# Overflow blocks of two mixture-of-experts layers: from one nest to groups of at most seven

## The reference, cut to what matters

```python
def hier_moe(xt, wg, bg, we, be, w1, w3, w2):
    # a group of 8 experts is chosen, in it the best TOP_K = 2 of 32 experts in all
    ...
    counts = jnp.bincount(flat_e, length=N_EXPERTS)
    ...
    def expert_block(args):
        xb, e = args
        hb = jax.nn.silu(xb @ w1[e]) * (xb @ w3[e])      # 1024 -> 512
        return hb @ w2[e]                                # 512 -> 1024
```

## Time and profile before

| | |
|---|---|
| median of 3 runs | 2109.87 us (2107.73 to 2110.74) |
| profiled execution, its own time | 2111.29 us |
| its span, first to last instruction | 2109.4 us |
| PE busy | 1954.9 us (93%) |
| DVE, ACT, POOL busy | 653.6, 370.9, 321.7 us |
| granted TensorE clock, mean | 0.992 |
| the chain that ended last | PE 69%, DMA 20%, DVE 3%, "issue" 3% |

### The profile page before, as it was taken

How to read it: one execution, slowest core, us unless ns; L and a number is a source line. 1 busy time by engine, 2 the same in 40 slices (tenths; PEclk the granted TensorE clock), 3 DMA queues, 4 the chain that set the end, 5 groups by cost and what they waited for, 6 DMA issues and landing times.

```text
span 2109.4 us, 34164 instructions
## 1 busy us (share of the span) xinstructions
PE 1954.9 (93%) x14831; PEld 1224.5 (58%) x14831; DVE 653.6 (31%) x1520; ACT 370.9 (18%) x821; POOL 321.7 (15%) x264
## 2 busy tenths in 40 slices
PE   5999999999999979999999888888789989989998
PEld 4566475555555546546565444444367677675884
DVE  1235273322222234114331111111146031037752
ACT  3133230000000002113320000000021130042131
POOL 0125402000001000114310000000120060040120
PEclk9999999999999999999999999999999999999999
DMA  9585199999999988317299999999984323427221
GB/s 362 124 274 205 56 357 381 427 426 427 426 427 422 426 347 261 118 52 281 95 381 426 427 427 426 427 426 426 407 293 151 131 81 135 145 81 200 81 92 60
DMA packets 133744, 586.23 MB, mean 278 GB/s; under 512 B 19162, under 2 KB 34474, under 8 KB 108880
## 3 DMA queue, kind: packets, MB, share of 16 engines
q1 hardware_dynamic: 117024, 558.65, 67.4%
q10 hardware_dynamic: 10448, 18.88, 3.0%
q0 software_dynamic: 6112, 6.39, 0.9%
HBM read 572.23 MB, written 25.29 MB: 283 GB/s over the span
## 4 chain that ended last, share of the span: by engine, by line
PE 69%; DMA 20%; DVE 3%; issue 3%; ACT 2%; POOL 2%; SPq 1%; DVEq 0%; POOLq 0%; ACTq 0%
DMA RG<-in_moe_w 19%; PE banks L1574 13%; PE banks L2627 8%; PE banks L1599 6%; PE banks L1550 4%; PE banks L2219 4%; PE banks L2629 4%; PE banks L1119 4%; PE banks L683 3%; PE banks L2221 3%; PE banks L2828 3%; PE banks L3039 2%; POOL AR L931 2%; PE banks L341 2%; PE banks L824 2%
## 5 line engine op out<-in xcount | busy, mean ns | idle before, releaser
L1574 PE MATMUL banks<-RG,HT 128*64 128x256 f32 x3616 | 427.8, 390 | 36.6 <-DMA RG<-in_moe_w 33.6
L1574 PEld LDWEIGHTS banks<-RG,HT 128*64 128x64 f32 x3616 | 252.6, 135 | 223.3 <-DMA RG<-in_moe_w 55.5
L1844 POOL DMA_INDIRECT y_rows<-AR x64 | 63.9, 999 | 839.8 <-DVE AR L1613 812.1
L1583 DVE TENSOR_TENSOR AR<-AR,banks 128x256 f32<-128x256 f32 x64 | 38.6, 603 | 479.6 <-ACT AR L1579 428.4
L1599 PE MATMUL banks<-RG,AR 128*64 128x512 f32 x752 | 171.7, 598 | 3.8 <-DVE AR L1592 3.1
L2627 PE MATMUL banks<-HT,RG 128*128 128x256 f32 x768 | 168.0, 380 | 0.8 <-ACT HT L550 0.8
L2627 PEld LDWEIGHTS banks<-HT,RG 128*128 128x128 f32 x768 | 145.4, 190 | 22.8 <-issue 2.4
L1579 ACT ACTIVATE AR<-banks 128x256 f32<-128x256 f32 x64 | 24.5, 383 | 744.6 <-PE banks L1574 744.6
L1550 PE MATMUL banks<-AR 128*128 128x256 bf16 (+1 forms) x1152 | 149.4, 277 | 2.0 <-DVE AR L1538 1.5
L1550 PEld LDWEIGHTS banks<-AR 128*128 128x128 bf16 x1152 | 108.3, 99 | 33.8 <-issue 18.3
L1599 PEld LDWEIGHTS banks<-RG,AR 128*64 128x64 f32 x752 | 50.0, 136 | 94.4 <-issue 83.4
(11 more groups left out here) (490 smaller groups left out, 2392.6 us busy)
## 6 DMA issues: line engine op xcount, KB each, us to landing
RG<-in_moe_w SPq DMA_DIRECT2D x160, 2048.0 KB
AR<-in_moe_w SPq DMA_DIRECT2D x32, 2048.0 KB, 21.5
RG<-in_ada_w SPq DMA_DIRECT2D x24, 2048.0 KB
RG<-in_attn_w_in SPq DMA_DIRECT2D x20, 2048.0 KB
RG<-in_odd_w_in SPq DMA_DIRECT2D x6, 2048.0 KB
RG<-in_ssm_w_in SPq DMA_DIRECT2D x4, 2048.0 KB
AR<-y_rows SPq DMA_DIRECT2D x12, 512.0 KB, 6.1
RG<-in_even_w_in SPq DMA_DIRECT2D x2, 2048.0 KB
```

Of the source, the lines that this page charges most:

```text
L1574: m = pe.matmul(p[64 * h:64 * h + 64, 256 * i:256 * i + 256], x[:, k, :], w[:, h, k], start=k == 0, stop=k == 7, skip_group_check=True)
L1844: g.indirect_dma_start(y, off, E.Y[b], None, bounds_check=2047, oob_is_err=False).then_inc(*event)
```

## The change

The nest is cut after every seventh block (`OVER = 7`). In layer 0 the 15 blocks become three nests, of 7, 7 and 1 blocks, one behind the other, each with an outer test of its own. The last block of a full group runs `over_end` without the inner test, since the code behind it is outside the nest. `sp_again` and the waits for it stand at the end of each group, inside its outer test, with a semaphore value of their own. In layer 1 there are 7 blocks, so one group, and the code is as it was. PE's part and SP's part in full:

```diff
+OVER = 7
 ...
         def pe_overflow(pe, E):
 ...
                     pe_down(pe, E, b, over_view(l, s2, 4), ev(f"over_pe{l}", "down", o))
-                    with pe.If(n < o + 2):
+                    if (o + 1) % OVER == 0:
                         over_end(pe, E, o)
-                    if o + 1 < E.no:
+                    else:
+                        with pe.If(n < o + 2):
+                            over_end(pe, E, o)
+                    if o + 1 < E.no and (o + 1) % OVER:
                         block(o + 1)
 
-            block(0)
+            for o in range(0, E.no, OVER):
+                block(o)
 ...
         def sp_overflow(sp, E):
 ...
-                    with sp.If(n < o + 2):
+                    if (o + 1) % OVER == 0:
                         over_end(sp, E, o)
-                    if o + 1 < E.no:
+                    else:
+                        with sp.If(n < o + 2):
+                            over_end(sp, E, o)
+                    if o + 1 < E.no and (o + 1) % OVER:
                         block(o + 1)
-                    if o == 0:
-                        sp_again(sp, E)
-
-            block(0)
+                    if o % OVER == 0:
+                        sp_again(sp, E, o)
+
+            for o in range(0, E.no, OVER):
+                block(o)
 ...
-        def sp_again(sp, E):
+        def sp_again(sp, E, o):
             for t in range(2):
-                sp.wait_ge(*at(f"z_load{t}", E.l, 1))
-                sp_z_load(sp, E, t, f"z_again{E.l}", t)
+                sp.wait_ge(*at(f"z_load{t}", E.l, 1) if o == 0 else at(f"z_again{E.l}{o - OVER}", 1, 1))
+                sp_z_load(sp, E, t, f"z_again{E.l}{o}", t)
```

More of the change, by code:

```diff
@@ L1937, in block @@
                     act_silu(act, E, b, ev(f"over_act{l}", "silu", o))
-                    with act.If(n < o + 2):
+                    if (o + 1) % OVER == 0:
                         over_end(act, E, o)
-                    if o + 1 < E.no:
+                    else:
+                        with act.If(n < o + 2):
+                            over_end(act, E, o)
+                    if o + 1 < E.no and (o + 1) % OVER:
                         block(o + 1)
-            block(0)
+            for o in range(0, E.no, OVER):
+                block(o)
         def dve_overflow(v, E):
@@ L1962, in block @@
                     dve_y_out(v, E, E.Y[b], b, ev(f"over_dve{l}", "y_out", o))
-                    with v.If(n < o + 2):
+                    if (o + 1) % OVER == 0:
                         over_end(v, E, o)
-                    if o + 1 < E.no:
+                    else:
+                        with v.If(n < o + 2):
+                            over_end(v, E, o)
+                    if o + 1 < E.no and (o + 1) % OVER:
                         block(o + 1)
-                    if o == 0:
-                        v.wait_ge(*at(f"z_again{l}", 1, 1))
-            block(0)
+                    if o % OVER == 0:
+                        v.wait_ge(*at(f"z_again{l}{o}", 1, 1))
+            for o in range(0, E.no, OVER):
+                block(o)
         def pool_overflow(g, E):
@@ L1983, in block @@
                             pool_gather(g, E, 34 + o, b, dm(f"over_gather{l}{b}", o + 2))
-                    if o == 0:
+                    if o % OVER == 0:
                         for t in range(2):
-                            g.wait_ge(*at(f"z_load{t}", l, 1))
+                            g.wait_ge(*at(f"z_load{t}", l, 1) if o == 0 else at(f"z_again{l}{o - OVER}", t, 1))
                     g.wait_ge(*at(f"over_dve{l}", "y_out", o))
                     pool_scatter(g, E, 32 + o, b, dm(f"over_store{l}{b}", o))
-                    with g.If(n < o + 2):
+                    if (o + 1) % OVER == 0:
                         over_end(g, E, o)
-                    if o + 1 < E.no:
+                    else:
+                        with g.If(n < o + 2):
+                            over_end(g, E, o)
+                    if o + 1 < E.no and (o + 1) % OVER:
                         block(o + 1)
-            block(0)
+            for o in range(0, E.no, OVER):
+                block(o)
         def over_view(l, slot, a):
```

## The result

| | before | after |
|---|---|---|
| median | 2108.80 us (2107.32 to 2110.74, 4 runs) | 2126.31 us (2122.06 to 2131.16, 4 runs) |
| profiled execution, its span | 2109.4 us | 2129.3 us |
| granted TensorE clock, mean | 0.992 | 0.983 |
| time ratio | | 1.0080, 95% interval 1.0068 to 1.0092 |

The change makes the kernel slower. The same kernel was timed once more in another set (first experiment) and took 2121.64 us, 12.6 more than the kernel before beside it. The forecast was 12.8 more, a time of 2122.7, in a range of 2115 to 2126.5.

What follows compares the result with a forecast made beforehand. PE, busy 93% of the span, bounds the kernel. Second jump 6.08, third 6.5, tests 0.1 and clock 0.5, less 0.4 slack, make 12.8 us more: 2122.7 us on the median of 2109.87, range 2115 to 2126.5.

Steps and rivals of the forecast that it cites:

- Where the cost lies: PE in layer 0 pays; DVE's and SP's stalls stay as they were, ACT and POOL nothing, layer 1 no change.
- First jump: PE's first outer test in layer 0, over seven blocks, into an idle queue: 3.83 us as before.
- Second jump: PE's second outer test in layer 0, over seven blocks, DMA engines full: 6.08 us, bounds 3.83 and 6.5.
- rival B: PE's second jump in layer 0 first awaits the piece behind the first's target: 19.3 us slower, 2129.2; chance 0.08.
- Third jump: PE's outer test of block 14 in layer 0 crosses a piece's start by 5 instructions: 6.5 us, bounds 0.05 and 6.5.
- Rival A: PE's third jump in layer 0 finds its target on hand: 5.8 or 3.5 us slower, 2113.4 to 2115.7; chance 0.25.
- Rival C: No slower: PE's second and third branches in layer 0 take under 0.2 us each, 2109.5 to 2110.1; chance 0.07.
- Clock and slack: Behind PE's jumps in layer 0, half clock costs 0.5 us (0 to 1); slack before L2117 hides 0.4.
- gap after 31 keeping matmuls: PE's keeping matmuls behind layer 0's jumps still stop after 31 of 72, the target 2 instructions earlier in the same piece.
- Places: In layer 0, L413's transposes at about 793.5 us and L2117's matmuls at about 805.
- Downstream: Behind L2117 nothing absorbs the delay; the DMA-bound stretch of layer 1's experts starts later by as much.

Runs made afterwards that it cites:

- PE nested again: The changed kernel with PE back in one nest, ACT, DVE, POOL and SP still in groups of seven: 1.1 us less than before, ratio 0.9996.
- eight instructions more: The changed kernel with two more keeping matmuls on PE ahead of its overflow tests in layer 0: 7.2 us more than before, ratio 1.0032.
- After again: The changed kernel, unaltered, timed once more in another set: 2121.64 us, 12.6 more than before, ratio 1.0054.
- groups of one: The kernel before with PE alone, in layer 0 alone, cut into fifteen groups of one block: 40.6 us more than before, one run.
- PE alone grouped: The kernel before with groups of seven on PE only, the other four engines in one nest: 11.3 us more than before, ratio 1.0046.
- eight and seven: The kernel before with PE alone in groups of eight and seven in layer 0 (`OVER = 8`): 7.2 us more than before, ratio 1.0032.

## Why the prediction was right

The mechanism held: the cost is PE's code, fetched at each jump whose target isn't on hand. That the sum of 12.8 came so close to the second set's 12.6 is partly luck: its terms were off by up to 1.7 us each, in both directions, and cancelled. That the first set's 2126.31 us lies in the range, 0.2 us below its end, is luck too: 17.5 us is 4.7 more than forecast, the two new stalls were only 0.6 longer than forecast in that set, and the range's upper end was made for longer stalls. Point by point:

- **Where the cost lies.** DVE, SP, ACT and POOL were forecast at nothing, shown by PE nested again. Layer 1 was forecast without change: its test takes 6.0 to 6.6 us in all these kernels, 6.08 in the earlier trace rows.
- **First jump** 3.8: 3.34 to 3.90.
- **Second jump**, the mis-sized term: 6.08 forecast from layer 1's row, 7.36 to 7.77 measured. Layer 1's jump starts with no fetch open; this one starts 3.9 us after the first, and the fetch that follows the first jump is underway beside its own. That is rival B in part: it had the two fetches in a row and gave the first a full 6.5 us, but they run side by side, and the far jump takes 1.7 to 2.4 us more than the near one's 5.69.
- **Third jump** 6.5: 5.76 to 5.84. The bound taken was the gap of the keeping matmuls; the near jump is cheaper. The two errors are +1.3 to +1.7 and -0.7, so the two new stalls together are 13.1 to 13.6 us where 12.6 were forecast.
- **Rival A** needed a third test that finds its target, and gave +5.8. With eight instructions more it came true, and the kernel took +7.2: A's sum with the second jump's right price of 7.36 is 7.1.
- **Rival C** is out: no second test over a missing piece was short. By the Trainium skill ("Advanced Engine Details and Errata", Control Flow Timing) a compare and branch is some 108 ns; PE's short ones take 219 to 378 ns here, so the row is higher, and the stalled ones show that no such figure covers them.
- **Clock and slack.** 0.5 was forecast for the clock and 0.4 gained from slack. The lower clock came, and stayed for 3.6 us after PE resumed, but it ran into something the forecast had wrong: the gap after 31 keeping matmuls, said to stay, isn't there. All 72 run in 9.62 us. The transposes and the first 32 of them take 5.72 us at a mean clock of 0.69. The next piece came 6.5 us after the resume in the earlier trace rows; here PE stops for only 0.1 us, at 799.5 and so 5.9 us after the resume. The slower matmuls reach the piece's start hardly before it is there:

```profile
793.78:799.50 5.72, 5.72 (x36) 5.72 (x36) 4.28 (x8) 1.15 (x2) 0.00 (x0) 0.69 1.05 387
799.50:804.11 4.61, 4.61 (x42) 4.57 (x42) 3.47 (x13) 1.45 (x4) 0.00 (x0) 1.00 1.06 388
```

  From the transposes to the diagonal's matmuls it takes 10.33 us, against 11.58 in the earlier trace rows. So 13.2 us of later transposes became 12.0 of later diagonal, where the forecast had 12.7 become 12.8.
- **Places.** L413 was forecast at about 793.5 and is at 793.78; L2117 at 805, and is at 804.11.
- **Downstream** nothing was to be absorbed. After again gives 11.9 us at the diagonal and 12.6 in the time, groups of one 41.1 and 40.6, one run. The weights that come late near 1192 us were not forecast; in the time of these kernels they can't be told apart. The first set's further 5 us are explained neither by the forecast nor by a run.

## What to carry to other kernels

Code that never runs has a place and a size: on an engine with a long program, count the instructions between a branch and its target, for one far jump can be cheaper than several, and a few instructions ahead of a test can move the start of a piece out of its jump. A stall on the chain that ended last may still be worth nothing (DVE's 5.67 us), when another engine arrives 0.4 us earlier; of all versions tried, only the one that gave the others work during the stall was faster than the kernel before by more than the noise, by 6.3 us for its four edits together. When a profiled execution is longer by more than the stage explains, compare the granted clock and the waits along both timelines and time the kernel again before giving the rest a cause.

## What the runs showed of the hardware

- A missing piece of PE's code costs 2.8 to 3.9 us when the DMA engines are idle or half idle as it is asked for, 5.6 to 6.6 when they are full, and 7.4 to 8.1 when a far jump follows another.
- A far jump costs one packet more than a near one, and the second far jump stalls over two packets, so the piece behind a target is fetched even when the next jump passes over it.
- The granted clock stood at 0.50 from 780.3 to 797.4 us in after, 3.6 us into the matmuls that followed the stalls. With 45.65 us of standing still (fifteen groups of one) it rose again 3.1 us into them, and the 72 keeping matmuls took 9.26 us; with far shorter stalls it took 4.9 us in PE alone grouped and 5.9 in eight and seven.
- DVE's stall vanished with 14 instructions more ahead of its test, so there too the place of the test counts, which one shift shows and no more. Its code comes in smaller packets, by the queue that isn't PE's: 0.31 MB in 38 are about 8 KB each, 128 instructions. That queue can't be DVE's alone, since 38 such packets hold 4,864 instructions and the trace has 1,843 of DVE.
